# Both token parts in one wide matmul for the rounded expert table, with the sum made by ScalarE and GpSimd

## What is computed

```python
def peer_ffn(h, wq, keys, u_tab, v_tab):      # retrieve, for a block of 128 tokens
    q = (xb @ wq).reshape(PEER_BLOCK, PEER_HEADS, 2, PEER_QDIM // 2)
    s = jnp.einsum('tphq,phkq->tphk', q, keys)
    top_s, top_i = lax.top_k(s, PEER_TOPK)
    ...                                        # best 16 of the 16 x 16 pairs: idx, and their softmax g
    act = jax.nn.gelu(jnp.einsum('tpkd,td->tpk', u_tab[idx], xb), approximate=False)
    return jnp.einsum('tpk,tpkd->td', g * act, v_tab[idx])
```

## Time and profile before

| | |
|---|---|
| median of 3 runs | 1585.44 us (1583.63 to 1587.64) |
| the profiled execution | 1587.25 us |
| its span | 1585.5 us, granted TensorE clock 0.997 |
| PE, DVE, ACT, POOL busy | 98%, 72%, 46%, 4% |
| first expert loop | from 787.3 us to 1217 us of the span |
| second expert loop | from there nearly to the end |

### The profile page before, as it was taken

One profiled execution on the slowest core, in us unless ns is written; L12 is line 12 of the kernel. 1 busy time (PEld: TensorE's weight loads), 2 busy tenths in 40 slices (PEclk: granted clock), 3 DMA queues, 4 the chain that ended last, 5 costly groups with the idle time before them and its releaser, 6 DMA issues.

```text
span 1585.5 us, 27790 instructions
## 1 busy us (share of the span) xinstructions
PE 1556.0 (98%) x10204; PEld 1385.1 (87%) x10204; DVE 1138.7 (72%) x2011; ACT 726.4 (46%) x1056; POOL 58.3 (4%) x107
## 2 busy tenths in 40 slices
PE   8999999999999999999999999999999999999997
PEld 7767776899999887889999999999999788888886
DVE  7993313477644877867599999998874777777776
ACT  5225212354433473334444655545454544545454
POOL 2002000010000014200000000000000000000000
PEclk9999999999999999999999999999999999999999
DMA  7363737545552321244287777755557777777774
GB/s 291 117 247 119 271 132 304 195 166 183 184 187 74 110 85 33 93 161 174 71 229 229 221 228 218 194 152 162 157 159 225 237 242 236 239 239 238 242 242 121
DMA packets 95937, 293.60 MB, mean 185 GB/s; under 512 B 10480, under 2 KB 45424, under 8 KB 82928
## 3 DMA queue, kind: packets, MB, share of 16 engines
q1 hardware_dynamic: 95712, 292.21, 57.4%
q10 hardware_dynamic: 144, 0.26, 0.0%
HBM read 274.60 MB, written 17.83 MB: 184 GB/s over the span
## 4 chain that ended last, share of the span: by engine, by line
PE 90%; DVE 5%; DMA 2%; ACT 1%; issue 1%; SPq 0%; DVEq 0%; POOL 0%; ACTq 0%; POOLq 0%
PE ps L437 90%; DVE split_ring L2013 1%; DMA ring<-in_peer_u 1%; DMA ring<-in_peer_v 1%; DVE big L1875 0%; DVE big L1337 0%; DMA ring<-in_w_gv 0%; DVE big L2062 0%; DMA kept_acts<-acts 0%; DVE big L2066 0%; DVE big L2064 0%; DMA x<-in_x 0%; DVE big L1541 0%; DVE hh L1646 0%; ACT split_ring L2571 0%
## 5 line engine op out<-in xcount | busy, mean ns | idle before, releaser
L437 PE MATMUL ps<-split_hh,split_ring 128*128 128x256 f32 x3296 | 409.7, 284 | 4.0 <-DVE split_ring L2013 2.8
L437 PEld LDWEIGHTS ps<-split_hh,split_ring 128*128 128x128 f32 x3296 | 399.7, 192 | 5.5 <-DVE split_ring L2013 1.9
L437 PE MATMUL ps<-split_ring 128*128 128x512 f32 (+1 forms) x1712 | 387.0, 384 | 4.8 <-DVE split_ring L2013 4.5
L437 PEld LDWEIGHTS ps<-split_ring 128*128 128x128 f32 x1712 | 313.4, 188 | 70.8 <-DVE split_ring L2013 8.7
L2013 DVE TENSOR_TENSOR split_ring<-ring,split_ring 128x1024 fp32r<-128x1024 f32 x256 | 311.8, 1220 | 50.3 <-ACT split_ring L2571 47.1
L2578 ACT ACTIVATE split_ring<-ring 128x1024 fp32r<-128x1024 f32 x128 | 135.9, 1062 | 175.6 <-DMA ring<-in_peer_v 175.6
L2571 ACT ACTIVATE split_ring<-ring 128x1024 fp32r<-128x1024 f32 x128 | 135.2, 1057 | 69.1 <-DMA ring<-in_peer_u 69.1
L437 PE MATMUL ps<-split_ffn_h,split_ffn_w 128*128 128x256 f32 x1056 | 127.4, 283 | 0.0
L437 PEld LDWEIGHTS ps<-split_ffn_h,split_ffn_w 128*128 128x128 f32 x1056 | 127.0, 192 | 0.1
L2122 DVE TENSOR_TENSOR split_ring<-ring,split_ring 128x256 fp32r<-128x256 f32 x128 | 54.4, 425 | 81.5 <-ACT split_ring L2585 81.4
L437 PE MATMUL ps<-split_hid_high,split_ffn_w 128*128 128x258 f32 (+1 forms) x736 | 111.7, 284 | 0.2
(11 more groups left out here) (329 smaller groups left out, 1729.7 us busy)
## 6 DMA issues: line engine op xcount, KB each, us to landing
ring<-in_peer_u SPq DMA_DIRECT2D x128, 512.0 KB, 3.9
ring<-in_peer_v SPq DMA_DIRECT2D x128, 512.0 KB, 3.7
ring<-in_w_mod SPq DMA_DIRECT2D x24, 1024.0 KB, 5.3
ring<-in_ffn_in SPq DMA_DIRECT2D x22, 1024.0 KB, 4.9
ring<-kept_acts SPq DMA_DIRECT2D x128, 128.0 KB, 3.5
ring<-in_ffn_out SPq DMA_DIRECT2D x11, 1024.0 KB, 4.9
ring<-in_w_out SPq DMA_DIRECT2D x8, 1024.0 KB, 7.2
ring<-in_peer_wq SPq DMA_DIRECT2D x8, 1024.0 KB, 7.7
```

Source lines behind the costliest of these rows:

```text
L437: return nc.tensor.matmul(out, lhsT, rhs, start=start, stop=stop, skip_group_check=True)
```

## The change

For slices 0 to 115 (`PAIRED` = 116) the rounded table moves both halves of `hh` in one matmul of 512 columns, so that the bank's first half holds high x high and its second half high x low; then 8 matmuls of 256 columns add low x high to the first half. ACT copies the whole bank to SBUF (`in_parts`, in the last 1024 columns of `big`), POOL adds the halves in place, and ACT takes the Gelu of the sum. On ACT the order for slice c becomes: copy of product c, Gelu of slice c-1, rounding of slice c+3. `s_read` now counts the copies, and the new flag `activations_ready` counts the Gelus; SP's store waits for the latter. The flags of the high and low parts of the two tables are merged into one each (`table_high_ready`, `table_split`), with 128 added to the counts of `peer_v`. PE waits for the rounded slice before the 8 wide matmuls, and for the low rest only before the 8 narrow ones. Slices 116 to 127 are as before.

```diff
+            def paired_activations(c, q, first_=False):
+                pe.wait_ge(table_high_ready, c + 1)
+                if not first_:
+                    pe.wait_ge(s_read, c - 1)
+                parts = ps[:, q % 2, :].rearrange("p (a t) -> p a t", a=2)
+                for k in range(KD):
+                    mm(parts, u_high[q][:, k * P:(k + 1) * P], split["hh"][:, :, k, :], k == 0, False)
+                pe.wait_ge(table_split, c + 1)
+                for k in range(KD):
+                    last = mm(ps[:, q % 2, 0:T], u_low[:, q, k * P:(k + 1) * P], h_high[:, k, :], False, k == KD - 1)
+                last.then_inc(s_made, 1)
...
-            def store_act(c, q):
-                sp.wait_ge(s_read, c + 1)
+            def store_act(c, q, paired=False):
+                sp.wait_ge(activated if paired else s_read, c + 1)
                 sp.dma_start(kept_acts[c], acts[q % 2]).then_inc(flag(f"act_out{q % 2}"), 16)
...
+            def next_activations(i, q, paired):
+                sp.wait_ge(s_made, 4 * i + (q + 1))
+                sp.dma_start(u_tile[:, q, :], d["peer_u"][4 * i + (q + 4)]).then_inc(flag(f"u_in{q}"), 16)
+                store_act(4 * i + q, q, paired)
+            with sp.Fori(0, PAIRED // 4) as i:
                 for q in range(4):
-                    sp.wait_ge(s_made, 4 * i + (q + 1))
-                    sp.dma_start(u_tile[:, q, :], d["peer_u"][4 * i + (q + 4)]).then_inc(flag(f"u_in{q}"), 16)
-                    store_act(4 * i + q, q)
+                    next_activations(i, q, True)
...
+            def keep_parts(c, q, first_=False):
+                act.wait_ge(s_made, c + 1)
+                if not (first_ and q < 2):
+                    act.wait_ge(flag("activations_ready"), c - 1)
+                a_(in_parts[:, q % 2, :], ps[:, q % 2, :], ACT.Copy).then_inc(s_read, 1)
+            def activate_added(c, q, i, first_=False):
+                act.wait_ge(flag("parts_added"), c + 1)
+                if not (first_ and q < 2):
+                    act.wait_ge(flag(f"act_out{q % 2}"), 32 * i + 16 * (q // 2))
+                a_(acts[q % 2], in_parts[:, q % 2, 0:T], ACT.Gelu).then_inc(flag("activations_ready"), 1)
+            def activate_paired(c, q, i, first_=False):
+                keep_parts(c, q, first_)
+                if not (first_ and q == 0):
+                    activate_added(c - 1, (q - 1) % 4, i - (q == 0), first_)
+                high_u(c + 3, (q + 3) % 4, i + (q + 3) // 4, first_ and q == 0)
...
+            def add_parts(c, q):
+                pool.wait_ge(s_read, c + 1)
+                both = in_parts[:, q % 2]
+                g.tensor_tensor(both[:, 0:T], both[:, 0:T], both[:, T:], ALU.add).then_inc(flag("parts_added"), 1)
```

More of the change, by code:

```diff
@@ L44 @@
 LAST = 3
+PAIRED = 116
 COLS = {}
@@ L300, in program @@
         h_high, h_low = split["hh"][:, 0], split["hh"][:, 1]
+        in_parts = big[:, NE * T - 4 * T:].rearrange("p (b n) -> p b n", b=2)
         mod_sum, mod_turned = ps[:, 4:7, :], ps[:, 7, 0:96]
@@ L1112, in _ @@
             e_ready, e_added = flag("weighted_ready"), flag("experts_added")
-            u_split, v_split = flag("u_split"), flag("v_split")
+            table_high_ready, table_split = flag("table_high_ready"), flag("table_split")
             def expert_weights(n, half, first_=False):
@@ L1124, in activations @@
             def activations(c, q, first_=False):
-                pe.wait_ge(u_split, c + 1)
+                pe.wait_ge(table_split, c + 1)
                 if not first_:
@@ L1133, in activations @@
                 last.then_inc(s_made, 1)
+            def paired_activations(c, q, first_=False):
[5 more added lines that the diff above has]
+                    mm(parts, u_high[q][:, k * P:(k + 1) * P], split["hh"][:, :, k, :], k == 0, False)
+                pe.wait_ge(table_split, c + 1)
+                for k in range(KD):
+                    last = mm(ps[:, q % 2, 0:T], u_low[:, q, k * P:(k + 1) * P], h_high[:, k, :], False, k == KD - 1)
+                last.then_inc(s_made, 1)
             def experts_in(c):
-                pe.wait_ge(v_split, c + 1)
+                pe.wait_ge(table_split, c + (NE + 1))
                 pe.wait_ge(e_ready, c + 1)
@@ L1180, in _ @@
             for q in range(4):
-                activations(q, q, q < 2)
+                paired_activations(q, q, q < 2)
             with pe.Fori(1, KEYS_AT // 4) as i:
                 for q in range(4):
-                    activations(4 * i + q, q)
+                    paired_activations(4 * i + q, q)
             turn_keys(0)
@@ L1194, in _ @@
                 for c in range(u_before(g), u_before(g + 1)):
-                    activations(c, c % 4)
+                    (paired_activations if c < PAIRED else activations)(c, c % 4)
             with pe.Fori(U_AT // 4, NE // 4) as i:
@@ L1260, in _ @@
             s_made, s_read, e_added = flag("activations_made"), flag("activations_read"), flag("experts_added")
+            activated = flag("activations_ready")
             def load_v(c, q):
@@ L1274, in _ @@
                 sp.dma_start(u_tile[:, q, :], d["peer_u"][q]).then_inc(flag(f"u_in{q}"), 16)
-            with sp.Fori(0, NE // 4 - 1) as i:
+            def next_activations(i, q, paired):
[3 more added lines that the diff above has]
+            with sp.Fori(0, PAIRED // 4) as i:
                 for q in range(4):
-                    sp.wait_ge(s_made, 4 * i + (q + 1))
-                    sp.dma_start(u_tile[:, q, :], d["peer_u"][4 * i + (q + 4)]).then_inc(flag(f"u_in{q}"), 16)
-                    store_act(4 * i + q, q)
+                    next_activations(i, q, True)
+            for i in range(PAIRED // 4, NE // 4 - 1):
+                for q in range(4):
+                    next_activations(i, q, False)
             sp.wait_ge(flag("expert_weights_made"), T // 4)
@@ L2011, in low_of @@
                 tile, high, low = (u_tile, u_high, u_low) if kind == "u" else (v_tile, v_high, v_low)
-                dve.wait_ge(flag(kind + "_high_ready"), c + 1)
+                dve.wait_ge(flag("table_high_ready"), c + (1 if kind == "u" else NE + 1))
                 v.tensor_tensor(low[:, q, :], tile[:, q, :], high[q].bitcast(F32), ALU.subtract)\
-                    .then_inc(flag(kind + "_split"), 1)
+                    .then_inc(flag("table_split"), 1)
             u_at = [0]
@@ L2570, in high_u @@
                     act.wait_ge(s_made, c - 3)
-                a_(u_high[q], u_tile[:, q, :], ACT.Copy).then_inc(flag("u_high_ready"), 1)
+                a_(u_high[q], u_tile[:, q, :], ACT.Copy).then_inc(flag("table_high_ready"), 1)
             def high_v(c, q, i, first_=False):
@@ L2577, in high_v @@
                     act.wait_ge(e_added, c - 3)
-                a_(v_high[q], v_tile[:, q, :], ACT.Copy).then_inc(flag("v_high_ready"), 1)
+                a_(v_high[q], v_tile[:, q, :], ACT.Copy).then_inc(flag("table_high_ready"), 1)
             def high_weighted(c, q, first_=False):
@@ L2599, in activated @@
                     for q in range(4):
-                        activate(4 * i + q, q, i)
+                        activate_paired(4 * i + q, q, i)
             def exp_weights_of(b):
@@ L2638, in _ @@
             for q in range(4):
-                activate(q, q, 0, True)
+                activate_paired(q, q, 0, True)
             activated(1, EXP_AT[0] // 4)
@@ L2652, in _ @@
                 for c in range(u_before(g), u_before(g + 1)):
-                    activate(c, c % 4, c // 4)
-            activated(U_AT // 4, NE // 4 - 1)
+                    if c < PAIRED:
+                        activate_paired(c, c % 4, c // 4)
+                    else:
+                        if c == PAIRED:
+                            activate_added(c - 1, 3, c // 4 - 1)
+                        activate(c, c % 4, c // 4)
+            for c in range(U_AT, NE - 4):
+                activate(c, c % 4, c // 4)
             for q in range(4):
@@ L2805, in _ @@
                                     channel_multiplier=-sign).then_inc(flag("att_ready"), 1)
+            s_read = flag("activations_read")
+            def add_parts(c, q):
+                pool.wait_ge(s_read, c + 1)
+                both = in_parts[:, q % 2]
+                g.tensor_tensor(both[:, 0:T], both[:, 0:T], both[:, T:], ALU.add).then_inc(flag("parts_added"), 1)
+            for q in range(4):
+                add_parts(q, q)
+            with pool.Fori(1, PAIRED // 4) as i:
+                for q in range(4):
+                    add_parts(4 * i + q, q)
 def blocks(w):
```

## The result

The changed kernel takes 1636.89 us, median of 4 runs (1635.36 to 1638.91), against 1585.48 before: 3.3% more (ratio 1.0328, 95% interval 1.0315 to 1.0341), 51 us. The forecast was 1624, with a range of 1597 to 1643. The profiled execution took 1637.01 us with a span of 1635.3. One of the ten runs of the experiment with both mends and doubled copies took 2061.39 us at a granted clock of 0.70, the slow state, and is left out of its ratio.

A forecast was written before the change was run, and what follows sets the result against it. PE set the pace before; after, a wait loop through DRAM was to bound the search part. +40.8 us there and -2 in the one-hot part, on a median of 1585.44, gave 1624 us; range 1597 to 1643.

The forecast's parts named there:

- the ring: Search part, 76 slices: chain Gelu, store, table load, rounding, copy, Gelu takes 6.62 us per two slices, over PE's 5.56.
- Matmuls: First expert loop: 8 wide and 8 narrow matmuls take 2.78 us a slice, 0.10 less than 2.88.
- the pace: Search part: three products at 2.78 us, then 73 slices at 3.31, 8.3 + 241.6, against 222.5 us before.
- Table loads and Exp: Search part on ACT: two Exps and eight table loads, one a turn of four, add 13.4 us in full.
- DVE's search and subtraction: Search part: DVE, busy 2.67 us a slice, follows with more room; its blocks holding PE for about 3 us vanish.
- One-hot part: The 44-slice part: PE stays the bound by very little; 4.0 us saved, 2 us lost on weight copies, net -2.
- The hidden load: Rival: table loads stay hidden, needing a landing under 2.94 us, and the change gains; 1574 us, 5 in 100.
- The port: Rival: DVE and GpSimd exclude each other, 3.41 us a slice in the search part; 1640 us, 12 in 100.
- The short ring: Rival: landings of 3.5 to 3.6 us and table loads in ACT's idle time; 1597 us, 14 in 100.
- What would show it: Search part: slice every 3.2 to 3.45 us, 3.6 with table loads; PE idle 0.5 us each; DRAM about 190 GB/s.

The follow-up runs named there:

- both mends and doubled copies: Changed kernel with the load ahead of the previous slice's store, a 128x1 Gelu behind each Exp, and each bank copied twice on ACT: 1580.28 us (0.9978).
- The wide matmuls alone: Kernel before with the 512-column matmul in all 128 slices, all else in the old order, high x low left out of the sum: 1576.66 us (0.9957).
- the doubled copies: Changed kernel with a small Gelu behind each Exp and each bank copied twice on ACT: 1637.45 us (1.0342).
- the run with Gelu's table kept: Changed kernel with an added Gelu of 128x1 behind each Exp, so the loops are entered with Gelu's table: 1613.46 us (1.0195).
- both mends: Changed kernel with the load ahead of the previous slice's store and a Gelu of 128x1 behind each Exp: 1582.01 us (0.9983).
- the load first: Changed kernel with SP issuing the load of slice c+4 behind product c and only then the store of slice c-1: 1589.03 us (1.0030).
- the run with the Gelu in the same turn: Changed kernel with a Gelu behind each Exp, SP's order as changed, and ACT making Gelu(c) directly after copy(c): 1616.41 us (1.0201).

## Why the prediction came out as it did

The direction, the place and the mechanism were right: 51 us where 39 were forecast, all of them in the part with the search. The size was less right than the total says: the ring turned faster than forecast and the table loads and Exps cost more, and the two errors in part cancel. By its own steps:

- *Matmuls.* The step said 0.10 us a slice. The wide matmuls alone gave 0.07 to 0.09, by how it is counted. The sign and the bounds held; the size was somewhat too high.
- *The ring.* The step said 6.62 us for two slices. It was 6.41, since the slices' loads landed in 3.33 to 3.73 us where I took 4.00 for them (median of the whole run 3.8). The copy and the Gelu came as taken (0.48 and 0.41 us, where I took 0.50 and 0.38). In us of the whole part the pace alone was forecast to give 8.3 + 241.6 - 222.5 = 27.4; at 3.20 us a slice it gives 8.3 + 233.6 - 222.5 = 19.4. The load moved ahead of the store removes it, the doubled copies move it by their dose in one order and not in the other: this cause is shown.
- *Table loads and Exp.* This is the term that was mis-sized: 13.4 us forecast, of which 8 x 1.28 = 10.2 for the loads in the loops and 3.2 for the two Exps. The loads cost 24.4. What is left of the 25.8 beside the pace, 6.4, lies around the two Exps: the slice with each took 6.5 and 6.8 us in place of 3.2 in the run with Gelu's table kept, where a small Gelu and its table load stand behind each Exp. I took the loads to stand where they stood, one to a turn. But a copy now comes first in the body of the loop, and gets a load of its own, 8 in all. Had I counted these 10.2 us, the forecast would have been 1634. That the loads lie on the ring with nothing to hide them was right; they cost even more than their length. In all, 19.4 + 6.4 + 24.4 = 50.2 us, where 27.4 + 3.2 + 10.2 = 40.8 were forecast.
- *DVE's search and subtraction.* I said that its holds of PE vanish. They did not: PE waited 6.8 us for DVE in the changed kernel's first part, 6.5 with both mends. In the changed kernel the chain of waits runs through DVE only once for long, from 874.97 to 881.67 us; what that cost no run separates. With the ring gone it counts.
- *One-hot part.* -2 forecast, -0.6 measured. Of the 3.1 that the wide matmuls give there 2.5 went again. The doubled copies, 5 us there, show how near the ring is to PE in it. But with the load first the part still takes 165.9 to 166.0 us, so the ring has at most 0.7 of the 2.5, and the rest is open.
- *The rivals.* The hidden load (1574) was wrong: the least landing was 3.3, and 2.94 was needed. The port (1640) came out near the measured time for the wrong reason: without any adds the kernel took 1635. It has a price, 10.9 us of DVE's time with both mends, and 6 of them are paid once the ring is gone. The short ring (1597) was out: its landings of 3.5 were nearly right, its hidden table loads not.
- *What would show it.* A slice every 3.2 us was right, but 4.0 and not 3.6 with table loads. PE's idle time was 37.5 us in the part, 0.5 a slice, as said, but by luck: a slice took 3.58 us on the mean with PE busy 3.08, where the forecast had 3.31 and 2.78. DRAM's traffic fell from 220 to 178 GB/s, further than the 190 written down. DVE waited for ACT's rounding 38 times, at half of the slices and not at nearly all.

## What to carry to other kernels

When a result is finished one turn later than before, look at every queue that waits for it in order: what stands behind that wait now waits too, here the next load behind a store. Follow the ring round once with durations from rows and compare it with the bound's own time for as many turns; a ring can be longer than each engine's work in it, and then decides while every engine has idle time. And when another function comes first in a loop's body on ScalarE, count the table loads again.

## What the runs showed of the hardware

- In these kernels ACT's loop entered behind an Exp loaded a table in each turn, at its Gelu, and with a copy ahead of the Gelu twice, 1.283 us each; slices 4 to 31, entered behind a Gelu, had no load. With a Gelu of 128x1 behind each Exp 1 of the 17 loads was left at these two lines, and one stands at each small Gelu.
- In the changed kernel and in the run with the Gelu in the same turn a GpSimd add of 128x256 took 1.29 us (the median) in place of 0.735. From 836 to 863 us of the changed kernel eight adds that start behind one of DVE's subtractions take 1.29 to 1.41 us; one starts ahead of it (859.34) and takes 0.74, and there the subtraction takes 1.68 in place of 1.22. With both mends it is mostly this way round: the adds took 0.74 us (the median of the first part), and the 75 subtractions 1.365 us on the mean in place of 1.218. The Trainium skill ("SBUF — State Buffer", section "Who interferes with whom") says that the later of two such instructions waits for the whole of the other. The trace agrees nearly: in the run with the Gelu in the same turn, the add at 842.38 took 1.41 - 0.735 = 0.68 us more, where 0.82 were left of the subtraction (841.99 + 1.21 = 843.20).
- With PE busy 234 of 272 us the mean granted clock of that stretch was 0.96 of full speed, where it was 1.00 before, with PE busy 219.6 of 221.2 us. PE wasn't the bound there.
